# A decoder layer on one core: weight remainders on VectorE two steps late, gathers on GpSimd, weighing ahead of turning

## What is computed

```python
def reference(x, mem, positions, ...):
    h = rmsnorm(x, attn_norm)
    proj = h @ w_in
    qkv_a, b_q, b_k, b_v, m_q = split(proj)
    o_a = dilated_mixture_attn(qkv_a, positions, ...)   # windows (128,1), (512,4), (2048,16)
    o_b = sink_swa_gqa(b_q, b_k, b_v, positions, ...)   # window 128, 8 query heads, 2 key heads
    o_m = memory_attn(m_q, mem, mem_norm, w_mem_kv, ...)
    gates = sigmoid(h @ w_gate + b_gate)
    x = x + (gates_a * (o_a @ w_o_a) + gates_b * (o_b @ w_o_b) + gates_m * (o_m @ w_o_m)) @ w_out
    return x + conv_ffn(rmsnorm(x, ffn_norm), w_up, conv_w, conv_b, w_down)
```

## Time and profile before

| | us |
|---|---|
| median of 3 runs | 1875.52 |
| lowest and highest | 1873.69, 1876.38 |
| profiled execution, its own time | 1876.01 |
| profiled execution, span | 1874.2 |
| TensorE busy in the span | 1777.5 (95%) |
| VectorE, GpSimd, ScalarE busy | 738.5, 639.5, 577.8 |

### The profile page before, as it was taken

How to read it: one execution, slowest core, us unless ns; L and a number is a source line. 1 busy time by engine, 2 the same in 40 slices (tenths; PEclk the granted TensorE clock), 3 DMA queues, 4 the chain that set the end, 5 groups by cost and what they waited for, 6 DMA issues and landing times. The chain is left out here.

```text
span 1874.2 us, 23271 instructions
## 1 busy us (share of the span) xinstructions
PE 1777.5 (95%) x8889; PEld 1443.6 (77%) x8889; DVE 738.5 (39%) x1320; ACT 577.8 (31%) x1059; POOL 639.5 (34%) x535
## 2 busy tenths in 40 slices
PE   4789998989989899999999998999999999999999
PEld 3577787767767778888888886888888888888887
DVE  4634435337885402210055232333423424342343
ACT  4434555534444422322121322311221221122121
POOL 5444545453342122222144632413321331332122
PEclk8899999999989999999999998999999999999999
DMA  5301102011210043332345602202201210220002
GB/s 188 107 17 35 35 2 56 15 34 26 68 35 1 1 116 90 100 103 90 102 157 164 217 1 67 68 23 67 67 22 45 67 45 22 67 67 21 24 23 90
DMA packets 118270, 119.28 MB, mean 64 GB/s; under 512 B 15340, under 2 KB 95916, under 8 KB 118188
## 3 DMA queue, kind: packets, MB, share of 16 engines
q1 hardware_dynamic: 118188, 118.16, 20.6%
HBM read 101.25 MB, written 16.89 MB: 63 GB/s over the span
## 5 line engine op out<-in xcount | busy, mean ns | idle before, releaser
L1890 PE MATMUL ps<-act_hi,f_hi 128*128 128x512 f32 x704 | 278.9, 396 | 6.3 <-DVE f_lo L1655 6.3
L1890 PE MATMUL ps<-act_hi,f_lo 128*128 128x512 f32 x704 | 276.8, 393 | 0.0
L1890 PE MATMUL ps<-act_lo,f_hi 128*128 128x512 f32 x704 | 274.5, 390 | 0.0
L1655 POOL TENSOR_TENSOR f_lo<-ffn_area,f_hi 128x1024 fp32r<-128x1024 f32 x65 | 155.3, 2419 | 87.7 <-ACT f_hi L1736 87.7
L1845 DVE TENSOR_TENSOR attn_out<-ps,attn_out 128x512 f32<-128x512 f32 x160 | 106.5, 687 | 136.4 <-PE ps L1910 136.3
L1890 PEld LDWEIGHTS ps<-act_hi,f_hi 128*128 128x128 f32 x704 | 133.2, 189 | 33.2 <-DVE f_lo L1655 6.7
L1890 PEld LDWEIGHTS ps<-act_hi,f_lo 128*128 128x128 f32 x704 | 132.8, 189 | 31.1
L1890 PEld LDWEIGHTS ps<-act_lo,f_hi 128*128 128x128 f32 x704 | 132.8, 189 | 29.3
L1555 PE MATMUL ps<-act_hi,g_hi 128*128 128x512 f32 x384 | 152.1, 396 | 3.1 <-DVE g_lo L1490 3.1
L1555 PE MATMUL ps<-act_hi,g_lo 128*128 128x512 f32 x384 | 151.2, 394 | 0.0
L1555 PE MATMUL ps<-act_lo,g_hi 128*128 128x512 f32 x384 | 149.9, 390 | 0.0
(11 more groups left out here) (220 smaller groups left out, 3751.9 us busy)
## 6 DMA issues: line engine op xcount, KB each, us to landing
ffn_area<-in_w_up_dram SPq DMA_DIRECT2D x44, 512.0 KB, 4.0
gates<-gate SPq DMA_DIRECT2D x24, 512.0 KB, 3.1
gate<-gates SPq DMA_DIRECT2D x24, 512.0 KB, 3.8
g_raw<-in_w_gate_dram SPq DMA_DIRECT2D x23, 512.0 KB, 4.6
ffn_area<-in_w_down_dram SPq DMA_DIRECT2D x22, 512.0 KB, 3.7
attn_out<-in_x_dram SPq DMA_DIRECT2D x16, 512.0 KB, 5.9
w_raw<-in_w_in_dram SPq DMA_DIRECT2D x16, 384.0 KB, 3.5
attn_out<-in_w_in_dram SPq DMA_DIRECT2D x16, 384.0 KB, 4.2
```

The lines of the kernel that those rows point to most:

```text
L1655: eng.tensor_tensor(f_lo[:, b, :], f_raw[b], f_hi[:, b, :].bitcast(F32), ALU.subtract).then_inc(f_lo_done[b], 1)
L1890: ins = pe.matmul(ps[:, 2 * q + half, :], w[:, q, k * P:(k + 1) * P], a[:, k, half * 512:(half + 1) * 512], start=(k == 0 and i == 0), sto ...
```

## The change

Four things are different. The two semaphores of the low parts are no longer one for even and one for odd slices but one for each engine. All low parts from slice 8 on are made on VectorE; GpSimd keeps the even ones of the first eight only. VectorE's low k stands at step k+2 of the last slot of a stage, and low 6 and low 7 so at steps 0 and 1 of the next slot. `gather_low` goes from VectorE's step 2 to GpSimd's end of slot. And TensorE weighs the values of unit n-3 ahead of turning the probabilities of unit n-2.

```diff
+def low_on_pool(n):
+    return n < 8 and n % 2 == 0
+
+def low_count(n):
+    on_pool = sum(low_on_pool(m) for m in range(n + 1))
+    return on_pool, n + 1 - on_pool
...
         def w_split(eng, n):
-            eng.wait_ge(w_lo_odd if n % 2 else w_lo_even, n // 2 + 1)
+            on_pool, on_dve = low_count(n)
+            eng.wait_ge(w_lo_pool, on_pool)
+            if on_dve:
+                eng.wait_ge(w_lo_dve, on_dve)
...
-                              ).then_inc(w_lo_odd if n % 2 else w_lo_even, 1)
+                              ).then_inc(w_lo_pool if low_on_pool(n) else w_lo_dve, 1)
+
+        def low_at(m):
+            if m < 8:
+                return None
+            at = last_job_of[m // 8 - 1] * 8 + m % 8 + 2
+            return at // 8, at % 8
...
         @block.gpsimd
-                for s in last_job_of:
-                    if last_job_of[s] == j and s + 1 < len(STAGES):
-                        for k in range(0, 8, 2):
-                            w_low(pool, 8 * (s + 1) + k)
+                if strided(j + 1):
+                    gather_low(j + 1)
...
         @block.vector
-                    if k == 2 and strided(j + 1):
-                        gather_low(j + 1)
                     if 0 <= j - 1 < NJ and k == TURN_AT[KIND[j - 1] == "B"]:
                         copy_k(j - 1)
-                    if k % 2 and j in last_job_of.values() and JOBS[j][0] + 1 < len(STAGES):
-                        w_low(dve, 8 * (JOBS[j][0] + 1) + k)
+                    for m in range(8 * len(STAGES)):
+                        if low_at(m) == (j, k):
+                            w_low(dve, m)
...
         @block.tensor
                         score(n)
+                        if n >= 3:
+                            weigh_values(n - 3)
                         if n >= 2:
                             turn_probs(n - 2)
-                        if n >= 3:
-                            weigh_values(n - 3)
```

More of the change, by code:

```diff
@@ L300, in input_projections @@
         raw_in = [sem(f"raw_in{n}") for n in range(8)]
-        w_hi_done, w_lo_even, w_lo_odd, w_used = (sem(n) for n in ("w_hi_done", "w_lo_even", "w_lo_odd", "w_used"))
+        w_hi_done, w_lo_pool, w_lo_dve, w_used = (sem(n) for n in ("w_hi_done", "w_lo_pool", "w_lo_dve", "w_used"))
         proj_done, sq_done, ss_done, rstd_done, normed, roped = (
@@ L577, in norm_and_rope, with gather_low @@
                                    ALU.add).then_inc(roped, 1)
+            def gather_low(j):
+                gather_from(pool, j)
+                pool.tensor_copy(gathered(j)[:, 1], columns(act_lo, j)).then_inc(lo_gathered, 1)
             for k in range(0, 8, 2):
@@ L855, in qk_job @@
                 return [j for j in range(NJ) if KIND[j] in QK_KINDS][i]
-            def gather_low(j):
-                gather_from(dve, j)
-                dve.tensor_copy(gathered(j)[:, 1], columns(act_lo, j)).then_inc(lo_gathered, 1)
             def copy_k(j):
```

## The result

| | before | after |
|---|---|---|
| median, us | 1875.67 (4 runs) | 1859.94 (4 runs) |
| lowest and highest | 1873.69, 1876.38 | 1855.45, 1865.13 |
| profiled execution: time, span | 1876.01, 1874.2 | 1865.13, 1863.3 |
| TensorE begins on the gates | 659.87 | 645.05 |

The ratio is 0.9919, with a 95% interval of 0.9891 to 0.9947. The kernel is 0.8% faster, 15.7 us; I had forecast 4.1 and a range of 1865.5 to 1879. The changed part gives 14.8 us by the start of the gates. The profiled execution is the slowest of its four: the part behind the gates, which the change leaves alone, took 1218.2 us in it and 1214.3 before.

The account below looks back on a forecast made before the run. TensorE, busy 95% of the span, was taken as the bound, leaving only idle time and slow clock. Terms 0 + 0.2 + 0.6 - 1.4 - 3.5 = -4.1 us gave 1871.9 profiled, 1871.4 median; range 1865.5 to 1879.

Parts of the forecast that it names:

- Weighing ahead of turning: TensorE's order within a unit: nothing late hangs on it; 0, bounds -1 and +1 us.
- A2 to B: Slots 27, 28: scores of step 4 start at 403.1, not 404.53, slow clock stays; -1.4 us, bounds -3 and 0.
- the load behind a low part: Slice load ahead of ScalarE's last cast at stage passages: takes 4.7 us after the low part, read from slot 27.
- A0 to A1: Slots 11, 12: old 4.07 us gap goes, new gap with slow clock opens; net +0.2 us, bounds -2 and +2.
- A1 to A2: Slots 19, 20: scores of step 4 1.15 us sooner, less 1.75 for slow clock; net +0.6, bounds -2 and +2.
- The new gaps: TensorE before the scores of step 4 in slots 12 and 20: 4 to 6 us, nearly 5 in slot 12.
- B to M: Slots 35, 36, VectorE the bound: waits for ScalarE go, two low parts move to slot 36; -3.5 us, bounds -6.5 and 0.
- the four waits of the earlier trace: Slot 35: VectorE's low parts waited 0.46, 0.76, 1.95 and 1.26 us for ScalarE's casts, 4.4 in all.
- Start: Slots 2, 4, 5: low 6 and 7 behind x tiles delay TensorE, slot 5 recovers it; net 0, bounds -1 and +5 us.
- slot 5 takes it back: Slot 4's step 6 comes 5.1 us late, but slot 5's turn only 1.4 late, with hardly a gap before it.
- The gather: 16 gathers moved to GpSimd's end of slot: 2.0 us each, fitting in 3.1 us there; cost 0.
- Rival (c): Loads come in time, no new gap at step 4 after slots 11, 19 and 27; about 1861 us, chance 0.15.

Follow-up runs that it names:

- the kernel without the delay: Changed kernel, but VectorE's low k stands at step k itself, not two steps later; 1856.65 us, ratio 0.9904.
- the kernels with late casts: Changed kernel, ScalarE's casts 6 and 7 moved behind next slot's squares: 1844.18 us; also low 6, 7 behind step 4's unit, memv and A0 kept in last slot: 1839.01.
- the other two orders: Kernel before with TensorE's unit ordered turn, scores, weigh: 1888.48 us (1.0072); or weigh, turn, scores: 1915.74 us (1.0231).
- kernel with full tiles: Changed kernel, but A-stage weighing matmuls use 128 columns of values instead of 64, with two VectorE copies out; 1865.78 us, ratio 0.9946.

## Why the prediction was wrong, step by step

- **Weighing ahead of turning** is the step that failed. It stood as "0, bounds -1 and +1" and measured -10.1 us alone (-7.5 by its trace, up to the gates). I had asked who waits for whom and found nobody, which was true. I had not looked at the idle of 0.17 us between TensorE's own groups, printed in the trace of before ahead of weighing and ahead of the projection in each of the 42 units of A that it holds whole, nor at how many changes of tile each order has. With the order alone the three middles of A are 1.3, 2.5 and 1.9 us shorter. That is 5.6 us before rounding, over 17 slots or 34 units, 0.16 us each, and as much for all 48 units of A would make 8. So most of the gain is seen, but the passages into A1 and A2 gained only 0.2 and 0.0, and the traces do not account for all of the 10.1. M has full tiles throughout and its slots gained nothing; B, where VectorE is the bound by the prediction's reading, gained 0.5.
- **A2 to B** was forecast at -1.4 and is -3.4 with the low parts and gathers alone. The mis-sized term is the load behind a low part, 4.7 us by the earlier trace rows. After, slice 7 is there 3.5 us after low 3 in slot 11 (179.84 + 0.95 to 184.25) and 3.3 in slot 27. That 4.7 was the long case of two in the trace of before: the loads of slices 6 and 7 landed 4.7 and 5.3 us after their issue in slot 27, but 3.3 and 3.4 in slot 11. In slot 27 they were issued 1.8 us behind those of slices 4 and 5 (392.14 against 390.34), in slot 11 2.6 us behind; whether that made the difference I didn't test.
- **A0 to A1 and A1 to A2** were forecast at +0.2 and +0.6 and are -0.9 and -0.7, and for these the same term was too long: counted from the start of the slot, the last cast of slots 11 and 19 ends 1.2 and 1.1 us sooner than I had it. The new gaps are 3.18 and 4.20 us, not nearly 5. The differences lie inside the bounds of 2 us.
- **B to M**, -3.5, is -3.1. The reading of the four waits of the earlier trace rows holds, and the kernel without the delay gives them back.
- **Start**, 0, is -1.0 with low parts and gathers alone and -0.5 in the whole change, with the starts forecast at 64.0, 92.2 and 105.5 measured at 64.30, 92.25 and 105.39. But "slot 5 takes it back" hid a cost: it is so only against the kernel before, and with low 6 and 7 ahead of the x tiles slot 6 begins 2.8 us earlier than in the changed kernel.
- **The gather**, 0 at 2.0 us each, is 2.04 to 2.23 us, and hidden in middle slots. That it depends on the other half of the change, GpSimd rid of its low parts, I had not said. The Trainium skill, GPSIMD Engine Reference, section 4.1 Engine selection, would have made it an estimated 1 us; the measurement decides for 2.
- **Rival (c)**, 1861, is nearest in time, and its mechanism did not happen: the new gaps opened. The time came near it by another way, the order. The gaps before the scores and those before the turns of slots 11 and 19 are gone together only in the kernels with late casts, and these take 1844 and 1839 us.

So the low parts and gathers gained 7.4 us where 4.1 was forecast, and the rest of the miss goes with the one term at zero.

## What to carry to other kernels

When a change reorders groups of matmuls, count the changes of tile in each order, and read the idle time ahead of each group's weight loads: a term is not zero because nobody waits. Keep an engine's in-order chain (here casts ahead of squares) free of steps that wait for a load; moving two casts behind the squares, with their low parts, brought as much as the whole change (15.8 us). And cost a move against the best place, not only against the old one: a stall that a later slot absorbs may still be worth moving.

## What the runs showed of the hardware

- Between groups of matmuls with different tiles the weight loads stand idle: 0.12 to 0.13 us out of the 64-row scores, 0.24 to 0.26 from the projection into the 64-row or 64-column group that follows it, and 0.17 at the other changes (A1, in the kernels before and after and in those with the other two orders). Between turning and projecting, which share a tile, there is none.
- Eight matmuls on 64 columns, alternating between the two halves of the array, take 0.42 us (kernel after), and on 128 columns 0.89 (kernel with full tiles).
- A copy of 128x1024 from fp32 to fp32r on GpSimd takes 2.04 to 2.23 us in the kernel after. A subtraction of 128x768 on VectorE takes 0.95 us alone and 2.23 to 2.77 beside it. In other kernels here the copy too is longer beside VectorE's low parts (2.73 and 2.80 us).
- A weight slice of 384 KB is on ScalarE 3.3 to 3.5 us after the low part that frees its place in slots 11 and 27 of the kernel after (3.9 in slot 19).
